# A streaming encoder layer: the down units placed behind the next row's first gate unit, and the first tiles' loads and splits cut into other pieces

## The chip, the cores and the metric

The kernel runs on one core of a Trainium2 chip. The time is device microseconds of that core for one execution, with inputs in HBM and outputs written back to HBM. The kernel before was timed in three runs. One further execution was taken by the profiler; all rows below are from that one.

## What is computed

One layer of a hybrid encoder is applied to 544 tokens: 512 of a prompt and 32 of a running stream. All values are float32, D_MODEL is 1024 and D_FF is 2816.

```python
def mixer(xn, conv_prev, w_in, ln_g, ln_b, w_s, b_s, conv_w, w_pa, w_pb, w_o):
    z = xn @ w_in
    u_a, v_a, bg, cg, hh, ga, gb = jnp.split(z, SPLIT_IDX, axis=-1)
    u = jax.nn.gelu(u_a, approximate=False)
    v = layernorm(jax.nn.gelu(v_a, approximate=False), ln_g, ln_b)
    a = u * spatial_gate(v, w_s, b_s)
...
    m = jax.nn.sigmoid(ga) * (a @ w_pa) + jax.nn.sigmoid(gb) * (bconv @ w_pb)
    return m @ w_o, xc[:, -(CONV_WIDTH - 1):], v

def swiglu(x, w_gate, w_up, w_down):
    return (jax.nn.silu(x @ w_gate) * (x @ w_up)) @ w_down

def trunk(x, ...):
        x = x + mo
        x = x + swiglu(rmsnorm(x, norm_ffn[l]), w_gate[l], w_up[l], w_down[l])
    return rmsnorm(x, norm_final), ...
```

The first product that runs is v_A = rmsnorm(x) @ W_in for the columns of v. The swiglu is the "ffn" and "down" phases of the kernel, and the last rmsnorm is its tail.

## The kernel before

**Layout.** Activations lie with features on the 128 partitions and the 544 tokens along the free dimension, in two halves of 272. Each float32 operand is split into a high part (`w_hi`, `act_hi`, made by a cast on ScalarE) and a low remainder (`w_lo`, `act_lo`, a subtraction on VectorE), and each product is three matmuls: high by high, high by low, low by high.

**Head.** SyncE issues, in this order, the scale columns `cols64`, the first block of x, and then pieces of the first weight unit between the other x blocks (`load_x`, `load_first`: four pieces of two 128-row blocks each, read from `w_in` in rows of 1 KB). ScalarE makes the high parts (`take_x`, `first_unit`) and VectorE the low ones. TensorE meanwhile runs `keep_busy(WARM)`: 14 matmuls of ones, each seen in the trace as two passes. Then it takes the K blocks one by one (`step(k, i, h)`): 12 matmuls for each block k. Each needs `x_ready` of that block and `first_lo` of the weights' piece.

**Units of seven products.** The projections behind the mixer and most of the feed-forward part run as units. A unit takes 1 MB of weights as four quadrants and forms seven products of sums of quadrants with sums of token halves and blocks (in place of eight). Each product is 4 blocks by 3 matmuls, so a unit is 84 matmuls. VectorE makes the sums of the weights (`sums_of_b`: one instruction at L1759 and two at L1763). ScalarE casts them (`form`, L1144), and VectorE subtracts (`form`, L1773). All forms of unit n+1 are made while TensorE works on unit n. ScalarE also copies the banks of products 0, 1, 2 and 4 out of PSUM (`copy_part`, L1155). TensorE needs these copies at products 2, 3, 4 and 6. Within a unit ScalarE's order is fixed: copy 0 and form 0, copy 1, copy 2 and form 2, form 3 where it stands alone, copy 4 and form 4, form 5, form 6. A copy behind a form waits for that form.

**The order of the feed-forward units** is the tuple `FFN`. There are 11 pairs of a gate unit and an up unit, in three rows of 4, 4 and 3 pairs (`PAIRS`). Behind each of the first two rows come four down units, which take that row's h = silu(gate) * up. The last row's down product is the separate phase "down". Units are numbered n = 0 to 29 here: 0 to 7 are the first row's gates and ups, 8 to 11 its downs, 12 to 19 the second row, 20 to 23 its downs, 24 to 29 the third row. h of a pair is turned into its seven operand forms during the next gate unit: the "split" work in `gate`, 8 instructions of VectorE between its own. A row's last pair has no gate behind it. Its eight instructions stand at the head of `down` for m = 0, and TensorE has a function of its own for that unit, `first_down`: it takes the known three blocks of products 0, 1 and 5 first, and then the fourth.

**From the feed-forward units to the phase "down".** At L2287 VectorE makes the low parts of the weights. Ahead of it stands a wait for `gf_all` (the final norm's weights, whose load waits for the last unit's `form_used`). ScalarE loads its table for the square root (L1488) ahead of its cast at L1477.

**Tail.** The last block of x is done in two token parts (`LAST`). For each part ScalarE squares (L1503), takes the root (L1505) and scales one row block (L1509). TensorE turns the block (L1008) and adds up the squares (L1024). VectorE ends the norm and scales the rest, and SyncE stores.

## Times and profile before

| | us |
|---|---|
| median of 3 runs | 856.38 |
| lowest and highest run | 855.93, 857.24 |
| the profiled execution | 856.78 |
| its span, first to last instruction | 854.7 |
| TensorE busy in it | 841.1 (98%) |
| VectorE busy | 700.1 (82%) |
| ScalarE busy | 448.2 (52%) |

The span leaves out 2.1 us of the profiled execution's time, which lie around it. In the trace a stretch where TensorE has nothing to run is idle time, with what ended it. The start of one matmul to the start of the next tells more exactly what was lost, since the ends are modelled.

### The profile page before, as it was taken

What the parts mean: (1) busy time and instruction counts of PE and PEld (TensorE: products, weight loads), DVE (VectorE), ACT (ScalarE), POOL (GpSimd) and SP (SyncE); (2) the same over time, 40 slices, a digit from 0 to 9 for tenths busy, and PEclk for the clock granted to TensorE, in tenths of its full rate; (3) what the DMA queues carried; (4) which work ended last, traced back from release to release, by engine and by line L of the source; (5) the groups of instructions that cost most, each with busy time, mean ns of one, the idle gap of its engine ahead of it and who ended that gap; (6) DMA issues with size and microseconds to landing.
All of it is one profiled execution on the core that took longest, in us unless ns stands there. A gap on an engine that the chain in (4) does not pass through costs nothing.

```text
span 854.7 us, 16297 instructions
## 1 busy us (share of the span) xinstructions
PE 841.1 (98%) x6654; PEld 837.7 (98%) x6654; DVE 700.1 (82%) x1098; ACT 448.2 (52%) x766; POOL 17.4 (2%) x23
## 2 busy tenths in 40 slices
PE   9999999999999999999999999999999999999996
PEld 9999999999999999999999999999999999999996
DVE  6768878789898989845578899999999999888545
ACT  7432225556566565651256776654566655466422
POOL 0000000000000000000000000000000000000031
PEclk9999999999999999999999999999999999999998
DMA  8333314132333232231542122222222222222322
GB/s 300 114 100 102 105 51 151 50 107 99 108 97 110 93 112 98 96 126 50 178 134 90 51 99 100 99 99 99 100 99 100 99 97 101 99 99 69 93 61 105
DMA packets 39496, 88.49 MB, mean 104 GB/s; under 512 B 2177, under 2 KB 28801, under 8 KB 33025
## 3 DMA queue, kind: packets, MB, share of 16 engines
q1 hardware_dynamic: 39424, 87.49, 30.3%
q8 instruction: 52, 0.85, 0.4%
q14 instruction: 20, 0.16, 0.1%
HBM read 85.10 MB, written 2.38 MB: 102 GB/s over the span
## 4 chain that ended last, share of the span: by engine, by line
PE 95%; DVE 2%; ACT 1%; DMA 0%; issue 0%; POOL 0%; DVEq 0%; ACTq 0%; POOLq 0%
PE ps_main L836 13%; PE ps_main L837 12%; PE ps_main L838 12%; PE ps_main L641 10%; PE ps_main L639 10%; PE ps_main L640 10%; PE ps_t L836 7%; PE ps_t L837 7%; PE ps_t L838 7%; PE ps_g L782 1%; PE ps_g L684 1%; DVE w_lo L1773 1%; ACT w_hi L1144 1%; PE ps_t L666 1%; DMA gf_all<-in_norm_final_dram 0%
## 5 line engine op out<-in xcount | busy, mean ns | idle before, releaser
L836 PE MATMUL ps_main<-xf_hi,w_hi 128*128 128x272 f32 x756 | 218.6, 289 | 0.0
L837 PE MATMUL ps_main<-xf_lo,w_hi 128*128 128x272 f32 x756 | 218.5, 289 | 0.0
L838 PE MATMUL ps_main<-xf_hi,w_lo 128*128 128x272 f32 x756 | 218.4, 289 | 0.0
L639 PE MATMUL ps_main<-act_hi,w_hi 128*128 128x272 f32 x692 | 201.1, 291 | 0.9 <-DVE w_lo L2287 0.9
L641 PE MATMUL ps_main<-act_hi,w_lo 128*128 128x272 f32 x692 | 200.0, 289 | 0.0
L640 PE MATMUL ps_main<-act_lo,w_hi 128*128 128x272 f32 x692 | 199.1, 288 | 0.0
L1773 DVE TENSOR_TENSOR w_lo<-w_sums,w_hi 128x1024 fp32r<-128x1024 f32 x150 | 129.6, 865 | 26.4 <-ACT w_hi L1144 25.7
L1144 ACT CAST w_hi<-w_sums 128x1024 fp32r<-128x1024 f32 x150 | 113.9, 760 | 57.4 <-DVE w_sums L1763 35.9
L836 PEld LDWEIGHTS ps_main<-xf_hi,w_hi 128*128 128x128 f32 x756 | 142.4, 188 | 0.0
L838 PEld LDWEIGHTS ps_main<-xf_hi,w_lo 128*128 128x128 f32 x756 | 142.3, 188 | 0.0
L837 PEld LDWEIGHTS ps_main<-xf_lo,w_hi 128*128 128x128 f32 x756 | 142.2, 188 | 0.0
L639 PEld LDWEIGHTS ps_main<-act_hi,w_hi 128*128 128x128 f32 x692 | 130.3, 188 | 1.3 <-issue 1.1
L640 PEld LDWEIGHTS ps_main<-act_lo,w_hi 128*128 128x128 f32 x692 | 130.4, 188 | 0.0
L641 PEld LDWEIGHTS ps_main<-act_hi,w_lo 128*128 128x128 f32 x692 | 130.1, 188 | 0.0
L836 PE MATMUL ps_t<-xf_hi,w_hi 128*128 128x272 f32 x420 | 121.6, 290 | 0.0
L837 PE MATMUL ps_t<-xf_lo,w_hi 128*128 128x272 f32 x420 | 121.4, 289 | 0.0
L838 PE MATMUL ps_t<-xf_hi,w_lo 128*128 128x272 f32 x420 | 121.3, 289 | 0.0
L1773 DVE TENSOR_TENSOR w_lo<-w_raw,w_hi 128x1024 fp32r<-128x1024 f32 (+1 forms) x104 | 95.9, 922 | 5.2 <-ACT w_hi L1144 4.9
L1144 ACT CAST w_hi<-w_raw 128x1024 fp32r<-128x1024 f32 (+1 forms) x104 | 83.9, 807 | 15.1 <-PE ps_t L838 9.7
L836 PEld LDWEIGHTS ps_t<-xf_hi,w_hi 128*128 128x128 f32 x420 | 79.1, 188 | 0.4
L838 PEld LDWEIGHTS ps_t<-xf_hi,w_lo 128*128 128x128 f32 x420 | 79.0, 188 | 0.0
L837 PEld LDWEIGHTS ps_t<-xf_lo,w_hi 128*128 128x128 f32 x420 | 79.0, 188 | 0.0
(281 smaller groups left out, 1288.6 us busy)
## 6 DMA issues: line engine op xcount, KB each, us to landing
w_raw<-in_w_quads_dram SPq DMA_DIRECT2D x20, 1024.0 KB, 4.9
w_raw<-in_w_gate_dram SPq DMA_DIRECT2D x11, 1024.0 KB, 4.9
w_raw<-in_w_up_dram SPq DMA_DIRECT2D x11, 1024.0 KB, 4.9
w_raw<-in_w_down_quads_dram SPq DMA_DIRECT2D x8, 1024.0 KB, 4.9
w_raw<-in_w_in_dram SPq DMA_DIRECT2D x6, 1024.0 KB, 5.1
w_raw<-in_w_pa_dram SPq DMA_DIRECT2D x4, 1024.0 KB, 5.4
w_raw<-in_w_pb_dram SPq DMA_DIRECT2D x4, 1024.0 KB, 5.2
w_raw<-in_w_o_dram SPq DMA_DIRECT2D x4, 1024.0 KB, 6.7
```

The source lines that it names most:

```text
L639: pe.matmul(out, whi, xhi, start=(opens and k == order[0]), stop=False)
L640: pe.matmul(out, whi, xlo, start=False, stop=False)
L641: last = pe.matmul(out, wlo, xhi, start=False, stop=(closes and k == order[-1]))
L666: last = pe.transpose(dst, src[:, c * P:c * P + ROWS[c]], ident[:, :])
L684: pe.matmul(ps_g[:, 1, 0:P], ones[:, :], ones[:, :], start=True, stop=True)
L782: pe.matmul(ps_g[:, 0, c * P:(c + 1) * P], tok[:, c, group], ws_t[:, g, :], start=True, stop=True)
L836: pe.matmul(out, whi, xhi, start=opens and k == 0, stop=False, skip_group_check=not opens)
L837: pe.matmul(out, whi, xlo, start=False, stop=False, skip_group_check=not opens)
L838: last = pe.matmul(out, wlo, xhi, start=False, stop=k == KQ - 1, skip_group_check=not opens)
L1144: act.copy(f_hi[:, form_group(q, f), :], form_source(q, f, s)).then_inc(third_hi if f == 3 else form_hi, 1)
L1773: dve.tensor_tensor(f_lo[:, group, :], form_source(q, f, s), fbits(f_hi[:, group, :]), ALU.subtract).then_inc(third_lo if f == 3 else form ...
```

## The change

The order of the feed-forward units becomes a function, `ffn_units`: each row's four down units now stand behind the **gate unit of the next row's first pair**, and the up unit of that pair behind them. So the row's last h is made in a gate unit, as that of every other pair. `first_down`, `parts_first` and the head of `down` for m = 0 are gone. The gate's result lies in `gate_sb` over the four down units.

At the head, x's first block is issued ahead of `cols64`, and both of its splits are done in two token halves. The first weights come in five pieces of 1, 1, 2, 2 and 2 blocks, from an input of their own that holds each partition's row in one piece. `WARM` goes from 14 to 9. One addition of squares moves behind a split.

Ahead of the phase "down", the wait for `gf_all` moves behind the first uses, and the first cast ahead of the table load. In the tail, ScalarE squares the second part ahead of scaling the first part's rows.

```diff
+def ffn_units():
+    order = []
+    for c, pairs in enumerate(PAIRS):
+        for n in range(pairs):
+            order.append(("gate", c, n))
+            if c and n == 0:
+                order += [("down", c - 1, m) for m in range(4)]
+            order.append(("up", c, n))
+    return tuple(order)
...
-    WARM = 14
+    WARM = 9
+    FIRST = ((0, 1), (1, 2), (2, 4), (4, 6), (6, 8))
...
-    ALONE = [0, QG] + [QG + n for n, (kind, _, m) in enumerate(FFN) if kind == "down" and m == 0]
+    ALONE = [0, QG]
...
             def load_first(n):
-                dst = w_raw[:, 0, n * 4 * P:(n + 1) * 4 * P].rearrange("p (k n) -> p k n", k=2)
-                src = row_blocks(w_in, slice(2 * n * P, 2 * (n + 1) * P), V0, 2 * P)
-                sp.dma_start(dst, src).then_inc(first_loaded[n], 16)
+                at = slice(FIRST[n][0] * 2 * P, FIRST[n][1] * 2 * P)
+                sp.dma_start(w_raw[:, 0, at], w_first[:, at]).then_inc(first_loaded[n], 16)
+            load_x(0)
             sp.dma_start(cols64[:], cols).then_inc(cols_loaded, 16)
-            load_x(0)
             load_first(0)
             load_x(1)
+            load_first(1)
             load_x(2)
-            load_first(1)
+            load_first(2)
...
+                weights(0)
+                for h in range(2):
+                    pe.wait_ge(x_ready, h + 1)
+                    for i in range(2):
+                        step(0, i, h)
+                for k in range(1, KD - 2):
+                    pe.wait_ge(x_ready, k + 2)
+                    weights(k)
...
+                def h_there(x, k):
+                    if k == KQ - 1:
+                        pe.wait_ge(hf_ready, h_made + {A11: 2, A12: 2, A22: 2, S3: 3, S1: 3, S2: 4, S4: 5}[x])
...
-                if kind == "down" and m == 0:
-                    first_down(QG + n, n % 2, c)
-                elif n >= 2:
+                if n >= 2:
                     seven(QG + n, n % 2, behind=...,
                           forms=h_forms if kind == "down" else x_forms,
+                          h_made=5 * (KQ * c + KQ - 1) if kind == "down" and m == 0 else None)
...
-                elif kind == "down" and m == 1:
+                elif kind == "down" and m == 0 and f == 2:
                     act.wait_ge(hf_ready, 5 * KQ * (c + 1))
...
-                split, plain = m and c < 2, m and c == 2
+                split, plain = n and (c < 2 or m == 0), m and c == 2
...
             act.wait_ge(silu_done, NF)
             act.activation(root[:, 0:1], msq[:, 0:1], ACT.Sqrt).then_inc(root_done, 1)
-            split_down(p, 0, 0, NF2)
...
-            dve.wait_ge(gf_loaded, 16)
             split_down(p, 0, 1, NF2)
             take_x2(0, 0, first=True)
             split_down(p, 0, 0, NF2)
             take_x2(0, 1, first=True)
+            dve.wait_ge(gf_loaded, 16)
...
+            last_squares(0)
+            last_root(0)
+            last_squares(1)
+            last_scale(0)
+            last_root(1)
+            last_scale(1)
```

In the changed kernel `split_down(p, 0, 0, NF2)` stands ahead of the `silu_done` wait. Between the last up unit of a row and the first down unit, VectorE's order is as follows. Before, from the last up unit's final form into the first down unit (`w_lo` and `w_sums` are a unit's forms and sums, `hf_lo` and `s_lo` are h's low parts):

```order
L2069 TENSOR_TENSOR up_sb<-ps_t,gate_sb 128x544
L2084 TENSOR_TENSOR gate_sb<-up_sb 128x544
L1773 TENSOR_TENSOR w_lo<-w_raw,w_hi 128x512
L2115 TENSOR_TENSOR hf_lo<-up_sb,hf_hi 128x272
L2090 SCALAR_TENSOR_TENSOR up_sb<-gate_sb,up_sb 128x272
L2108 TENSOR_TENSOR hf_lo<-up_sb,hf_hi 128x2x272
L2122 TENSOR_TENSOR hf_lo<-gate_sb,hf_hi 128x2x272
L2098 SCALAR_TENSOR_TENSOR up_sb<-up_sb 128x272
L2129 TENSOR_TENSOR hf_lo<-up_sb,hf_hi 128x272
L2136 TENSOR_TENSOR s_lo_121<-up_sb,s_hi_117 128x272
L1773 TENSOR_TENSOR w_lo<-w_sums,w_hi 128x512 x2
L1759 TENSOR_TENSOR w_sums<-w_raw 128x1024
```

After, the same place, now a gate unit:

```order
L2075 TENSOR_TENSOR up_sb<-ps_t,gate_sb 128x544
L1765 TENSOR_TENSOR w_sums<-w_raw 128x1024
L2090 TENSOR_TENSOR gate_sb<-up_sb 128x544
L1779 TENSOR_TENSOR w_lo<-w_raw,w_hi 128x512
L2112 TENSOR_TENSOR hf_lo<-up_sb,hf_hi 128x2x272
L1769 TENSOR_TENSOR w_sums<-w_sums,w_raw 128x512
L2096 SCALAR_TENSOR_TENSOR up_sb<-gate_sb,up_sb 128x272
L2119 TENSOR_TENSOR hf_lo<-up_sb,hf_hi 128x272
L1769 TENSOR_TENSOR w_sums<-w_sums,w_raw 128x512
L2102 SCALAR_TENSOR_TENSOR up_sb<-up_sb 128x272
L1779 TENSOR_TENSOR w_lo<-w_sums,w_hi 128x1024
```

The sums of the next unit's weights (L1759, now L1765) stood behind h's whole chain and now stand ahead of it, with the rest of the chain between them.

On VectorE at the head of the program, before (the splits of x, `act_lo`, and of the first weights, `w_lo`):

```order
L1563 SCALAR_TENSOR_TENSOR act_lo<-resid,cols_61,act_hi 128x544
L1569 TENSOR_TENSOR w_lo<-w_raw,w_hi 128x512
L1563 SCALAR_TENSOR_TENSOR act_lo<-resid,cols_61,act_hi 128x544 x2
L1569 TENSOR_TENSOR w_lo<-w_raw,w_hi 128x512
L1563 SCALAR_TENSOR_TENSOR act_lo<-resid,cols_61,act_hi 128x544 x2
```

and after:

```order
L1566 SCALAR_TENSOR_TENSOR act_lo<-resid,cols_61,act_hi 128x272
L1572 TENSOR_TENSOR w_lo<-w_raw,w_hi 128x256
L1566 SCALAR_TENSOR_TENSOR act_lo<-resid,cols_61,act_hi 128x272
L1566 SCALAR_TENSOR_TENSOR act_lo<-resid,cols_61,act_hi 128x544
L1572 TENSOR_TENSOR w_lo<-w_raw,w_hi 128x256
L1566 SCALAR_TENSOR_TENSOR act_lo<-resid,cols_61,act_hi 128x544
L1572 TENSOR_TENSOR w_lo<-w_raw,w_hi 128x512
```

The first matmul needs the first two of these rows in both kernels. Each of them is now half as wide, and the third block's weights come two rows later.

On ScalarE in the tail, before (squares, root, scaled rows, for the first part and then for the second):

```order
L1503 ACTIVATE y_sq<-x_last 128x256
L1505 ACTIVATE root<-msq 128x2
L1509 ACTIVATE y_tok<-y_tok,rstd 128x1024
L1503 ACTIVATE y_sq<-x_last 128x288
L1505 ACTIVATE root<-msq 128x3
```

and after:

```order
L1492 ACTIVATE y_sq<-x_last 128x256
L1498 ACTIVATE root<-msq 128x2
L1492 ACTIVATE y_sq<-x_last 128x288
L1505 ACTIVATE y_tok<-y_tok,rstd 128x1024
L1498 ACTIVATE root<-msq 128x3
```

The second part's squares, for which TensorE waits, moved ahead of one scaling of 1024 columns.

## Rows read from the trace of the kernel before

**Rows 1.** The profile's first line.

```profile
span 854.7 us, 16297 instructions
```

**Rows 2.** Waits of TensorE: engine line waited for: total us, times, longest.

```profile
PE ps_main L836 <- ACT parts L1155: 3.1, 2, 1.6
...
PE ps_main L639 <- DVE w_lo L2287: 0.9, 1, 0.9
...
PE ps_main L1024 <- ACT y_sq L1503: 0.4, 1, 0.4
```

**Rows 3.** Timeline of TensorE (start, us, line): first matmuls of units 8 to 11, 19, 20.

```profile
564.97 0.29 PE L836 MATMUL ps_main<-hf_hi,w_hi 128*128 128x272 f32 x1
...
577.69 0.29 PE L836 MATMUL ps_t<-hf_hi,w_hi 128*128 128x272 f32 x1
...
588.40 0.29 PE L836 MATMUL ps_main<-hf_hi,w_hi 128*128 128x272 f32 x1
...
598.97 0.29 PE L836 MATMUL ps_t<-hf_hi,w_hi 128*128 128x272 f32 x1
...
683.69 0.29 PE L836 MATMUL ps_t<-xf_hi,w_hi 128*128 128x272 f32 x1
...
694.47 0.29 PE L836 MATMUL ps_main<-hf_hi,w_hi 128*128 128x272 f32 x1
```

**Rows 4.** Timelines of VectorE (first sums) and ScalarE, units 5 to 10.

```profile
537.07 1.22 DVE L1759 TENSOR_TENSOR w_sums<-w_raw 128x1024 f32<-128x1024 f32 x1
...
546.26 1.22 DVE L1759 TENSOR_TENSOR w_sums<-w_raw 128x1024 f32<-128x1024 f32 x1
...
558.44 1.22 DVE L1759 TENSOR_TENSOR w_sums<-w_raw 128x1024 f32<-128x1024 f32 x1
...
574.68 1.05 ACT L1144 CAST w_hi<-w_sums 128x1024 fp32r<-128x1024 f32 x1 [2.72 <-DVE w_sums L1763]
575.63 0.39 ACT L1155 ACTIVATE parts<-ps_main 128x272 f32<-128x272 f32 x1
...
582.94 1.22 DVE L1759 TENSOR_TENSOR w_sums<-w_raw 128x1024 f32<-128x1024 f32 x1
...
593.19 1.22 DVE L1759 TENSOR_TENSOR w_sums<-w_raw 128x1024 f32<-128x1024 f32 x1
```

**Rows 5.** Timelines of the head, by engine.

```profile
0.82 0.40 SPq L510 DMA_DIRECT2D cols<-in_cols_dram  x1
...
1.69 6.03 PE L684 MATMUL ps_g<-ones 128*128 128x128 f32 x28 [1.69 <-POOL ident L2413]
...
7.48 0.37 PE L694 MATMUL ps_main<-act_hi,w_hi 128*128 128x272 f32 x1
...
4.24 0.75 ACT L1051 ACTIVATE act_hi<-resid,cols 128x544 fp32r<-128x544 f32 x1 [1.94 <-DMA resid<-in_x_t_dram]
5.76 0.62 ACT L1058 CAST w_hi<-w_raw 128x512 fp32r<-128x512 f32 x1 [0.77 <-DMA w_raw<-in_w_in_dram]
...
7.58 0.75 ACT L1051 ACTIVATE act_hi<-resid,cols 128x544 fp32r<-128x544 f32 x1 [0.38 <-DMA resid<-in_x_t_dram]
...
6.42 0.69 DVE L1569 TENSOR_TENSOR w_lo<-w_raw,w_hi 128x512 fp32r<-128x512 f32 x1 [0.52 <-ACT w_hi L1058]
...
9.07 0.69 DVE L1569 TENSOR_TENSOR w_lo<-w_raw,w_hi 128x512 fp32r<-128x512 f32 x1
```

**Rows 6.** Timelines around the start of the phase "down".

```profile
808.02 0.39 PE L639 MATMUL ps_main<-act_hi,w_hi 128*128 128x272 f32 x1 [0.89 <-DVE w_lo L2287]
...
804.14 1.28 ACT L1488 ACT_TABLE_LOAD   x1
...
806.92 0.96 DVE L2287 TENSOR_TENSOR w_lo<-w_raw,w_hi 128x768 fp32r<-128x768 f32 x1 [2.04 <-DMA gf_all<-in_norm_final_dram]
```

**Rows 7.** The tail: stretches, busy us by engine, clock, DMA share, GB/s.

```profile
850.00:851.00 1.00, 0.00 (x0) 0.00 (x0) 0.78 (x2) 0.45 (x1) 0.00 (x0) 0.67 0.64 240
851.00:852.00 1.00, 0.00 (x0) 0.00 (x0) 0.00 (x0) 0.00 (x0) 0.00 (x0) 0.50 1.06 402
```

More of the change, by code:

```diff
@@ L81 @@
 PAIRS = (4, 4, 3)
-FFN = tuple((kind, c, n) for c, pairs in enumerate(PAIRS)
-            for kind, n in [(kind, n) for n in range(pairs) for kind in ("gate", "up")] + [("down", n) for n in range(4 if c < 2 else 0)])
+def ffn_units():
[7 more added lines that the diff above has]
+    return tuple(order)
+FFN = ffn_units()
 class Phase:
@@ L704, in first_unit @@
                             step(k, i, h)
-                pe.wait_ge(first_lo, KD // 2)
+                weights(KD - 2)
                 for i in range(2):
@@ L825, in h_forms, with product @@
                 return (s4_hi[k][:], s4_lo[k][:]) if x == S4 else (hf_hi[:, x, k, :], hf_lo[:, x, k, :])
-            def product(q, s, f, blocks, forms, there=None, opening=(0, 1), used=1):
+            def product(q, s, f, blocks, forms, there=None):
                 _, _, x, bank = PRODUCTS[f]
-                out, opens = banks[s][bank], f in opening
+                out, opens = banks[s][bank], f < 2
                 for k in blocks:
@@ L838, in product, with seven @@
                     last = pe.matmul(out, wlo, xhi, start=False, stop=k == KQ - 1, skip_group_check=not opens)
-                if blocks[-1] == KQ - 1 and used:
-                    last.then_inc(form_used, used)
-            def seven(q, s, first=None, behind={}, bank_b=None, forms=x_forms):
+                last.then_inc(form_used, 1)
+            def seven(q, s, first=None, behind={}, bank_b=None, forms=x_forms, h_made=None):
                 def there(x, k):
                     pe.wait_ge(xf_ready, NPROD * (first + k) + X_ORDER.index(x) + 1)
+                def h_there(x, k):
+                    if k == KQ - 1:
+                        pe.wait_ge(hf_ready, h_made + {A11: 2, A12: 2, A22: 2, S3: 3, S1: 3, S2: 4, S4: 5}[x])
                 for f in range(NPROD):
@@ L1451, in seven @@
                             up_free(n, f)
-                        copy_part(q, s, f, first=parts_first[:] if kind == "down" and m == 0 else None)
+                        copy_part(q, s, f)
                     else:
@@ L2224, in up @@
                 second_sums(q, 1, up_sb)
-                if not last and QG + n + 1 in ALONE:
-                    next_form(n, 3)
                 second_rest(q, 1, up_sb)
@@ L2229, in up @@
                 scale_second(q, up_sb, gate_sb[:, 1, :], h_made)
-                if not last and QG + n + 1 not in ALONE:
+                if not last:
                     next_form(n, 4)
```

169 lines of the change are left out of this document (64 added, 105 removed).

## The prediction

> **What bounds the kernel now.** First the span [rows 1] against TensorE's busy time: 841.1 of 854.7 us. TensorE is the bound, and its matmuls stay the same in number and shape apart from the warm-up. So only its gaps count, and the work ahead of its first real matmul and behind its last. Second, who made it wait [rows 2]: two long waits for ScalarE's copy at L1155, one for VectorE's weights at L2287, one for the squares at L1503. Third, the timeline of TensorE, by the starts of whole units, since a lost interval shows there in full. A down unit without trouble takes 598.97 - 588.40 = 10.57 us [rows 3], or 84 matmuls at 0.126 us. The first down unit takes 577.69 - 564.97 = 12.72 us; the one of the second row has the same length, so there are two. Fourth, why it does [rows 4]: in the first down unit VectorE works off the eight instructions of h before it makes the next unit's sums. ScalarE's cast of these sums starts at 574.68, 9.71 us into the unit, after idling 2.72 us for them. The copy of product 4 stands behind that cast and ends at 576.02, and TensorE has waited for it since 574.5. That is the 1.55 us of the long wait; short waits for h's parts make up the rest.
>
> **The change, part by part.**
>
> *Down units behind a gate unit.* Removed: 12.72 - 10.57 = 2.15 us, twice, 4.30 us. What is late next? VectorE is nearly full here, so I follow when it starts a unit's sums, measured from TensorE's start of that unit. Its own pace comes from the distances of L1759 [rows 4]: from an up unit to the gate 546.26 - 537.07 = 9.19 us, from a gate with h's work to the up 558.44 - 546.26 = 12.18, from down to down 593.19 - 582.94 = 10.25. In unit 7 (start 564.97 - 10.62 = 554.35) the sums start at +4.09. The new gate unit has the work of the old ones. With units of 10.6 us, its sums start at 4.09 + 9.19 - 10.6 = +2.7, those of the first down unit behind it at 2.7 + 12.18 - 10.6 = +4.3. Each further down gains 0.3. Which lateness costs? Before, down unit 9 has +5.25 (582.94) and takes 588.40 - 577.69 = 10.71 us, so it loses 0.14. Unit 10 has +4.79 (593.19) and takes 10.57, so it loses nothing [rows 3, 4]. At +4.3 the new first down is inside, and the 0.14 goes too. The up unit ahead of the second row's downs took 694.47 - 683.69 = 10.78 us, 0.21 too long, with one form cast by itself which now falls away. The second row enters some 0.15 later than the first (two cycles of 9.19 + 12.18 against two of 10.6, over four pairs, less what idle time takes back), so at about +4.5, still inside. Sum: 4.30 + 0.14 + 0.21 = **4.65 us**. The addition of `parts_first` (one of 272 columns) falls away on VectorE and was hidden. The loads on SyncE's queue keep their number and their waits. Down unit 0 now puts its copies into the upper half of `up_sb`, where h lay, so ScalarE's copy of product 2 waits for h's last low part. By the split work's place in the gate before, that ends about 2 us into the down unit, and the copy's data exist at 4.5 us. If it were late, the forms behind it on ScalarE, and then TensorE, would be late by the same.
>
> *Start of the phase "down".* VectorE waited 2.04 us for `gf_all` and TensorE 0.89 us for VectorE [rows 6]. Without that wait, the next bound is ScalarE's cast. It now stands ahead of the table load of 1.28 us at 804.14, so it ends at about 804.14 + 0.82 = 805.0, and VectorE's 0.96 us ends at 806.0. TensorE wants the weights at about 807.0. Nothing is late. The gain is 0.89 us, and at most 1.1 with the slower restart (a first matmul of 0.39 us). I take **1.0**. The table load moves into ScalarE's idle time ahead of the second cast, and `gf_all`, there by 806.9, is first used some 6 us later.
>
> *Tail.* The squares of the second part no longer stand behind the scaling, so TensorE's last wait of 0.4 us [rows 2] goes. The scaled rows are ready about 0.9 us later and the root right behind them just in time. The stores, though, fill the DMA engines: they are at 0.64 from 850 to 851 and full after that [rows 7]. The last stores can come forward only into that 0.36 us. Bounds 0 and 0.45, value **0.3**.
>
> *Head.* The first matmul starts at 7.48 [rows 5]. Its chain was: piece 0 landed at 5.76, cast 0.62, low part from 6.42 in 0.69, that is 7.11, then the end of the 28 warm-up passes (6.03 us from 1.69). In the new kernel x's first block is issued 0.46 us sooner (at 0.82, the place of `cols64`). Piece 0 holds half, and the time from block to piece, 5.76 - 4.24 = 1.52, may halve, so it lands between 4.5 and 5.3. Half-width splits cost between half and all of 0.62 and 0.69; by their halves the first matmul can start at about 5.6, and 6.5 is the other bound. The 18 passes end at 1.69 + 18/28 x 6.03 = 5.6. But that is not the gain. TensorE next needs the third block's weights, which arrive in the same order and amount of data as before: low part at 9.07 + 0.69 = 9.76, and ScalarE was already waiting for data at 7.58 (0.38 us). They can be earlier by 0 to 0.46. TensorE reached that block at 7.48 + 24 x 0.126 = 10.5. So the head gains 10.5 - 9.76 = 0.7 to 1.2 us, and I take **0.95**; what comes earlier is spent waiting ahead of block 1 or 2. Block 0 in two halves adds one instruction each to ScalarE and VectorE, some 0.1 us of cover that is there. The moved addition of squares only lets a weight split go first.
>
> The warm-up's passes took 6.03 / 28 = 0.215 us each, while the real matmuls of twice their columns run at 0.126 from 7.7 on: the array was at 1.2 GHz until about then and at 2.4 GHz after it. The new kernel starts real work while it may still be at 1.2 GHz. Until 7.5 this costs nothing that counts, since 24 matmuls fit between 5.6 and 9.6 with half of that time at the lower level. By the Trainium skill's page "TensorE: Matmul & The Clock Gate" (Part 1: The HAM clock gate), the lower clock is the default state and only activity releases it, so a shorter warm-up with a gap behind it may delay the release. This speaks against `WARM` 9; what it would give is the first rival below.
>
> **Sum.** 4.65 + 1.0 + 0.3 + 0.95 = 6.9 us. The profiled execution took 856.78, its span being 854.7, so it would take 849.9 with a span of 847.8. It was 0.4 above the median of 856.38. Against the median the forecast is **849.5 us**.
>
> **Rivals.** (1) *The clock rises late.* A gap between the 18 passes and the first matmul leaves the array at 1.2 GHz until past block 1. The 24 matmuls then take 24 x 0.25 = 6.0 us from 5.6, block 2 starts at 11.6 rather than 10.5, and the head loses 1.1 in place of gaining 0.95: 851.5. For it: the first piece may land 0.8 us later than I take. Against: the work is nearly unbroken from 1.69. (2) *The stall moves.* If the gate with h's work behind a full row leaves VectorE later than my +4.3, the first downs pay what lies beyond +4.8, and at the +7.3 of the old first down all of the 4.3 comes back: 853.8; at +5.3, some 0.3: 849.8. For it: 12.18 is longer than a unit. Against: 9.19 ahead of it. (3) *Slower.* VectorE becomes the bound over the down units: their 10.25 us cycle (with the scaling of `resid` in the first row) stands only 0.32 below the unit's 10.57. If the new order (gate result to scale, copies in the other buffers) made each of the eight downs wait as long as the old first one, 1.55 us, that is 12.4 us: 849.5 + 12.4 = 861.9. It turns the change into a loss from 6.9 / 8 = 0.86 us per down unit on, a cycle of 11.4. Nothing in the rows shows such a cycle. (4) *The head does nothing*, because data land as late as before: 850.5.
>
> **How the numbers follow.** Forecast with its small variants 0.68 (848.4 to 850.6), rival 1 0.11, rival 2 0.10, rival 3 0.03, rival 4 0.08. The range goes from 848.2 (head 1.2, start of "down" 1.1, tail 0.45, and runs that differ by 0.6) to 851.8, past rivals 4 and 1. Below 0.2% (1.7 us, about what a measurement can tell from no change) falls nearly nothing. Faster 0.96, same 0.01, slower 0.03.
>
> **What would show it.** In the changed kernel's trace: the first matmul at 5.4 to 6.5, and the third block's at 9.3 to 9.8, with a gap ahead of block 1 or 2 (else rival 1 or 4); all units of the feed-forward part at 10.6, the two first downs too, and the sums of a first down at about +4.3 (rival 2 if beyond +4.8); no wait of TensorE at the start of "down"; the last squares right behind VectorE's last block, and stores with no gap between them. The prediction is wrong if a wait for a copy at the old L1155 remains in a down or gate unit, or if the blocks 2 to 7 of the head come in later than before.

## The result, and the profile after

| | before | after |
|---|---|---|
| median, us | 856.38 | 852.13 |
| lowest and highest of 5 runs | 855.93, 857.24 | 851.88, 852.22 |
| ratio of the medians, 95% interval | | 0.9949 (0.9935 to 0.9962) |
| span of the profiled execution | 854.7 | 850.1 |
| first matmul on x's squares, from the start ("head") | 25.67 | 26.21 |
| from there to the first matmul of the last block ("middle") | 812.84 | 807.04 |
| from there to the end ("tail") | 16.22 | 16.85 |

The kernel is 4.25 us faster. Forecast were 6.9, so 852.13 lies just above the range of 848.2 to 851.8. The three parts of the span say where: the middle gained 5.80 (forecast 4.65 + 1.0 = 5.65), the head lost 0.54 (forecast: a gain of 0.95), and the tail lost 0.63 (forecast: a gain of 0.3). The two marks of the changed kernel:

```profile
26.21 0.59 PE L738 MATMUL ps_t<-r_x,ones 128*128 128x512 f32 x1
...
833.25 0.36 PE L986 MATMUL ps_main<-act_hi,w_hi 128*128 128x256 f32 x1
```

**The middle.** TensorE's waits, to be read against [rows 2]:

```profile
PE ps_g L697 <- POOL ident L2401: 1.7, 1, 1.7
PE ps_main L707 <- DVE w_lo L1572: 0.8, 1, 0.8
PE ps_g L998 <- DVE x_last L2332: 0.5, 1, 0.5
PE ps_g L688 <- ACT r_diag L1344: 0.2, 1, 0.2
```

The waits for copies, for the weights of "down" and for the last squares are gone. One is new: 0.8 us for `w_lo`, and it lies in the head. The first matmuls of the gate unit 8, of down units 9 and 10, of the up unit behind them, and of down units 21 and 22 (TensorE's timeline, as in [rows 3]):

```profile
565.49 0.29 PE L858 MATMUL ps_main<-xf_hi,w_hi 128*128 128x272 f32 x1
...
576.08 0.29 PE L858 MATMUL ps_t<-hf_hi,w_hi 128*128 128x272 f32 x1
...
586.65 0.29 PE L858 MATMUL ps_main<-hf_hi,w_hi 128*128 128x272 f32 x1
...
618.35 0.29 PE L858 MATMUL ps_t<-xf_hi,w_hi 128*128 128x272 f32 x1
...
703.09 0.29 PE L858 MATMUL ps_t<-hf_hi,w_hi 128*128 128x272 f32 x1
...
713.66 0.29 PE L858 MATMUL ps_main<-hf_hi,w_hi 128*128 128x272 f32 x1
```

The two first downs take 586.65 - 576.08 = 10.57 and 713.66 - 703.09 = 10.57 us, where they took 12.72. All four downs of the row take 618.35 - 576.08 = 42.27 = 4 x 10.57, and the gate unit ahead takes 10.59. VectorE's first sums of these two units, and ScalarE's cast of the first ones:

```profile
580.34 1.21 DVE L1765 TENSOR_TENSOR w_sums<-w_raw 128x1024 f32<-128x1024 f32 x1
...
707.53 1.22 DVE L1765 TENSOR_TENSOR w_sums<-w_raw 128x1024 f32<-128x1024 f32 x1
...
582.78 1.05 ACT L1138 CAST w_hi<-w_sums 128x1024 fp32r<-128x1024 f32 x1 [1.51 <-DVE w_sums L1769]
```

The sums come at +4.26 and +4.44 (forecast +4.3 and +4.5), the cast at +6.70, against +9.71 before [rows 4]. At the start of "down" the cast (799.91) now stands ahead of the table load (800.76), VectorE's low part is done at 801.74, and TensorE's matmuls follow each other at 0.126 us throughout.

Cut at the first matmul behind the feed-forward units (802.45 before, 798.33 after), the middle shows its two terms apart. From the squares to that matmul it takes 776.78 us before and 772.12 after, a gain of 4.66 (forecast 4.65). From there to the last block it takes 36.06 and 34.92, a gain of 1.14 (forecast 1.0, at most 1.1). That matmul before, and after:

```profile
802.45 0.29 PE L639 MATMUL ps_main<-act_hi,w_hi 128*128 128x272 f32 x1
```

```profile
798.33 0.29 PE L652 MATMUL ps_main<-act_hi,w_hi 128*128 128x272 f32 x1
```

**The head.** SyncE's first issues, and the weights' pieces on ScalarE and VectorE up to TensorE's third block (to be read against [rows 5]):

```profile
0.82 0.40 SPq L515 DMA_DIRECT2D resid<-in_x_t_dram  x1
1.28 0.42 SPq L523 DMA_DIRECT2D cols<-in_cols_dram  x1
1.75 0.42 SPq L520 DMA_DIRECT2D w_raw<-in_w_first_dram  x1
...
3.93 0.52 ACT L1041 ACTIVATE act_hi<-resid,cols 128x272 fp32r<-128x272 f32 x1 [1.63 <-DMA cols<-in_cols_dram]
4.94 0.41 ACT L1048 CAST w_hi<-w_raw 128x256 fp32r<-128x256 f32 x1 [0.48 <-DMA w_raw<-in_w_first_dram]
...
9.55 0.62 ACT L1048 CAST w_hi<-w_raw 128x512 fp32r<-128x512 f32 x1 [1.38 <-DMA w_raw<-in_w_first_dram]
...
10.20 0.69 DVE L1572 TENSOR_TENSOR w_lo<-w_raw,w_hi 128x512 fp32r<-128x512 f32 x1 [1.17 <-ACT w_hi L1048]
```

```profile
5.86 0.59 PE L707 MATMUL ps_main<-act_hi,w_hi 128*128 128x272 f32 x1
6.25 0.43 PE L708 MATMUL ps_main<-act_lo,w_hi 128*128 128x272 f32 x1
6.47 0.43 PE L709 MATMUL ps_main<-act_hi,w_lo 128*128 128x272 f32 x1
...
9.93 0.29 PE L709 MATMUL ps_main<-act_hi,w_lo 128*128 128x272 f32 x1
11.04 0.36 PE L707 MATMUL ps_main<-act_hi,w_hi 128*128 128x272 f32 x1 [0.82 <-DVE w_lo L1572]
```

The first matmul starts at 5.86, 1.6 us sooner than before. But the third block's weights reach ScalarE at 9.55, after a wait of 1.38 us for data, and are ready at 10.89. Before that was 9.76. TensorE has finished two blocks by 10.06 and starts the third at 11.04. What the early start won is spent waiting, and half a microsecond more.

**The tail.** VectorE's last scalings, then the stores (their sizes and the median time from issue to landing):

```profile
843.70 1.53 DVE L2373 TENSOR_SCALAR y_tok<-y_tok,rstd 128x512 f32<-128x512 f32 x3 [0.27 <-DVE rstd L2363]
...
out_dram<-y_tok SPq DMA_DIRECT2D x3, 512.0 KB, 3.4
out_dram<-y_tok SPq DMA_DIRECT2D x2, 256.0 KB, 2.8
out_dram<-y_tok SPq DMA_DIRECT2D x1, 128.0 KB, 4.1
```

Before, these stores took 3.3, 2.2 and 3.2 us. And ahead of the scalings VectorE is idle for 0.27 us with its own result at hand.

### The profile page after: what moved, and what is told of

It reads as the page before. It is cut to its first block, busy times and chain, and to the rows that moved or that the text cites. A ratio compares the mean times of both kernels' runs of the same rounds, so it can differ in the third digit from the quotient of the medians.

```text
span 850.1 us, 16275 instructions
## 1 busy us (share of the span) xinstructions
PE 838.9 (99%) x6644; PEld 836.4 (98%) x6644; DVE 698.8 (82%) x1096; ACT 448.7 (53%) x766; POOL 18.1 (2%) x23
## 4 chain that ended last, share of the span: by engine, by line
PE 97%; DMA 1%; ACT 1%; DVE 0%; SPq 0%; issue 0%; DVEq 0%
PE ps_main L858 13%; PE ps_main L859 13%; PE ps_main L860 13%; PE ps_main L654 10%; PE ps_main L652 10%; PE ps_main L653 10%; PE ps_t L858 7%; PE ps_t L859 7%; PE ps_t L860 7%; PE ps_g L804 1%; DMA w_raw<-in_w_first_dram 1%; PE ps_t L679 1%; PE ps_g L679 0%; PE ps_main L707 0%; PE ps_main L709 0%; PE ps_main L708 0%
## 5 line engine op out<-in xcount | busy, mean ns | idle before, releaser
L1779 DVE TENSOR_TENSOR w_lo<-w_raw,w_hi 128x512 fp32r<-128x512 f32 (+1 forms) x102 | 95.6, 937 | 5.1 <-ACT w_hi L1138 4.8
L1138 ACT CAST w_hi<-w_raw 128x512 fp32r<-128x512 f32 (+1 forms) x102 | 83.5, 819 | 16.8 <-PE ps_t L860 10.8
```

Of the source, the lines that this page charges most:

```text
L1138: act.copy(f_hi[:, form_group(q, f), :], form_source(q, f, s)).then_inc(third_hi if f == 3 else form_hi, 1)
L1779: dve.tensor_tensor(f_lo[:, group, :], form_source(q, f, s), fbits(f_hi[:, group, :]), ALU.subtract).then_inc(third_lo if f == 3 else form ...
```

## The experiments

Kernels of one group ran on one chip, with runs of the kernel before between them. The kernel before itself, timed in group 4 once more as a kernel of its own, came out at a ratio of 1.0005 (0.9996 to 1.0014), its median 0.46 us from that of its own runs. So differences under half a microsecond between medians mean little by themselves. The marks inside the profiled executions are finer for the middle and the tail: the changed kernel's two executions (the first one and `e0_after_again`) agree there to 0.01 us, and the two of the kernel before to 0.30 in the middle and 0.01 in the tail. Of the head that isn't so. The same two differ by 0.35 us there (26.21 and 25.86), and the two of the kernel before by 0.56 (25.67 and 25.11).

**Group 1: the changed kernel again, the whole head undone, and its parts.** `e0_after_again` is the changed kernel. `e1_head_before` takes back the head:

```diff
-            load_x(0)
             sp.dma_start(cols64[:], cols).then_inc(cols_loaded, 16)
+            load_x(0)
-    WARM = 9
-    FIRST = ((0, 1), (1, 2), (2, 4), (4, 6), (6, 8))
+    WARM = 14
+    FIRST = ((0, 2), (2, 4), (4, 6), (6, 8))
-            take_x(0, slice(0, HALF))
+            take_x(0)
             first_unit(0)
-            take_x(0, slice(HALF, N))
-                sp.dma_start(w_raw[:, 0, at], w_first[:, at]).then_inc(first_loaded[n], 16)
+                sp.dma_start(dst, row_blocks(w_in, slice(k0 * P, k1 * P), V0, 2 * P)).then_inc(first_loaded[n], 16)
```

`e3_rows_of_w_in` has only the last of these edits. `e4_four_pieces` has only the four pieces, in before's order among the x blocks.

> The changed kernel itself once more, as the measure for the others of this set. If what its first profile showed is the kernel's own: the third block's weights land at about 9.5 us, its first matmul starts at about 11.0, TensorE reaches the sum of x's squares at 26.2 (25.7 before), and the span ends 8.7 us after the last squares are summed (7.6 before). If the late landing and the long stores were chance of one execution, block 3 starts at 9.3 to 9.8 and the time is 849.5 to 850.5.

> The changed kernel with the whole head of before: the scale columns first, four pieces of two blocks in 1 KB rows of w_in, x's first block split whole, 14 warm-up matmuls. Theory that the new head costs 0.5 us: the first matmul at 7.5, no wait behind it, the squares' sum reached at 25.7, time 0.5 us below the changed kernel (851.6). Rival, that the head is neutral and the shift comes with the execution: no difference over 0.2 us.

> The changed kernel with its five pieces read from w_in in 1 KB rows, all else as changed. Theory that the new layout of the source makes the landings late (rows of one 8 KB row per partition, 2 KB per packet): the third block's weights land at 8.0 to 8.3 in place of 9.5, its matmuls start at 9.5 to 9.8, time 1.2 us below the changed kernel (850.9). Rival, that order and number of the pieces do it: still 9.3 to 9.6, time within 0.3 us of the changed kernel. Theory of the clock: no difference either.

> The changed kernel with four pieces of two blocks each from the new input, x's first block still ahead of the scale columns and split in halves. Theory of the layout: the second piece still lands after 9 us, time within 0.3 us of the changed kernel. Rival, the extra DMA and the queue position of the third block's piece (3.63 in place of 3.20): it lands 0.4 to 1.3 us sooner than 9.5, and the time is 0.4 to 1.2 us below the changed kernel, though the first matmul comes 0.4 us later.

| kernel | median (range), us | third block starts | head | tail |
|---|---|---|---|---|
| before, same chip | 856.29 | | | |
| e0, changed kernel | 851.86 (851.75 to 851.98) | 10.70 | 25.86 | 16.85 |
| e1, head of before | 850.62 (850.28 to 850.99) | 9.94 | 25.04 | 16.46 |
| e3, first weights from `w_in` | 851.16 (850.97 to 851.79) | 10.61 | 25.77 | 16.87 |
| e4, four pieces | 852.90 (851.16 to 854.47) | 10.61 | 25.70 | 16.47 |

The new head as a whole costs 851.86 - 850.62 = 1.24 us: 0.82 in the head and, unforeseen, 0.39 in the tail. Reading from `w_in` gives 0.70 of that back in the median; its profiled execution was its slowest (851.79), so its marks show little of it. The first piece with 256 KB from the new input is worse than with 128: its cast starts at 6.08, against 4.94 in e0 and 4.99 in e1, whose piece has 256 KB too but comes from `w_in`. Single runs of e4 lie up to 3.3 us apart.

**Group 2: before's head plus one of the new edits.** Each is e1 with one thing more: `e5_x_first` issues x's first block ahead of `cols64`, `e6_five_pieces` takes five pieces from `w_in`, `e7_warm_9` has 9 warm-up matmuls. `e9_head_tail_before` has before's order of ScalarE in the tail too:

```diff
             last_squares(0)
             last_root(0)
-            last_squares(1)
             last_scale(0)
+            last_squares(1)
```

> The changed kernel with the head of before (which gave 850.6), and of the new head only x's first block issued ahead of the scale columns. Theory that the order of the first two DMAs upsets the loads behind them: the third block starts at 10.3 or later in place of 9.9, the squares' sum is reached at 25.5 or later in place of 25.0, time 851.0 to 851.5. Rival, that the number of pieces does it: x's first block is cast 0.3 to 0.45 us sooner, nothing later, time within 0.2 us of 850.6.

> The changed kernel with the head of before, and of the new head only the five pieces of 1, 1, 2, 2 and 2 blocks (in 1 KB rows of w_in). Theory that the fifth DMA delays the third block's piece and, by the stores' place on the DMA engines, the end: third block at 10.4 or later, the end 8.7 us after the last squares in place of 8.3, time 851.2 to 851.9. Rival of the order of x and the columns: third block at 9.9, time within 0.2 us of 850.6.

> The changed kernel with the head of before, and of the new head only 9 warm-up matmuls in place of 14. Theory of the data: the first matmul waits for the first piece all the same and starts at 6.5, time within 0.2 us of 850.6. Rival of the clock: the array stays at its lower level for longer (0.226 us a matmul in blocks 0 and 1), the squares' sum comes up to 1 us later, time 851.0 to 851.6.

> The changed kernel with the head and ScalarE's tail order of before. Theory that the new tail order saves the wait of 0.5 us but the stores bunch up: the last squares come 0.5 us later (8.64 us after the last block's start in place of 8.13), the end is 7.6 us behind them in place of 8.3, time 0.2 us below 850.6. Rival, that the long stores come from an instruction load among them and not from the order: the end stays 8.3 us behind them, time 0.5 us above 850.6.

| kernel | median (range), us | first matmul | head | tail |
|---|---|---|---|---|
| e5, x first | 851.14 (850.57 to 851.33) | 6.97 | 25.18 | 16.46 |
| e6, five pieces | 850.74 (850.49 to 851.50) | 6.52 | 24.98 | 16.47 |
| e7, `WARM` 9 | 850.32 (850.28 to 850.58) | 6.62 | 24.84 | 16.47 |
| e9, before's tail order | 850.75 (850.44 to 851.49) | 6.82 | 25.04 | 16.64 |

None of the three costs 0.8 us by itself. e6 has the third block's weights as in the changed kernel, behind one piece more and issued at 3.63 rather than 3.20, and its third block starts at 9.61, sooner than e1's. The shorter warm-up is no loss. The new order of the tail is worth 16.64 - 16.46 = 0.18 us here, which a median can't show.

**Group 3: pairs, and the halves.** `e8_halves` is e1 with the token halves kept. `e10_x_first_five` is e5 and e6 together, `e11_five_warm_9` e6 and e7 together. `e12_whole_x` is the changed kernel with only the halves undone.

> The changed kernel with the head of before (first weights from w_in in four pieces, the scale columns first, 14 warm-up matmuls), except that the splits of x's first block stay in two token halves. Theory A (the halves carry the loss: ScalarE's and VectorE's extra pieces stand ahead of the later blocks, and the tail's instructions come 0.25 us later): x's squares sum at 25.4 to 25.9 (25.04 in e1), last sums to the end of the span 8.7 us in place of 8.3, median 851.3 to 851.8. Theory B (the halves cost nothing by themselves, the loss comes from the first piece of 128 KB together with x issued ahead): within 0.25 of e1's 850.6, the sum of squares at 25.0, last sums to the end 8.3.

> The changed kernel with before's head, except for two of the new edits together: x's first block issued ahead of the scale columns, and five pieces of 1, 1, 2, 2, 2 blocks (read from w_in). x's first block is split whole, 14 warm-up matmuls. Theory A (x first, by itself +0.5 us against e1, is what delays the pieces; five pieces only bring weights earlier): the sum of x's squares at 25.1 to 25.3, median 851.0 to 851.3. Theory B (the two edits hurt only together, the small first piece being taken early and the third block's weights late, with a wait ahead of block 2): third block at 10.3 or later, median 851.4 to 851.9. If the halves are the cause, it stays at 850.6 to 851.0.

> The changed kernel with before's head, except for 9 warm-up matmuls and five pieces read from w_in. Alone these gave 850.32 and 850.74 where the plain head of before gave 850.62. Theory A (each moves the first matmuls a little, and the third block's weights at 9.3 to 9.4 are early enough in both): 850.2 to 850.6, first matmul 6.4 to 6.6, third block 9.5 to 9.8, sum of x's squares at 24.8 to 25.0. Theory B (a short warm-up with an early first piece keeps the array at the lower clock longer, as in the changed kernel): blocks 0 and 1 at 0.2 us a matmul or more until about 7.8, third block at 10.0 or later, 850.9 to 851.5.

> The changed kernel with one edit undone: x's first block is split whole, not in token halves. All the rest of the new head stays (x first, 9 warm-up matmuls, five pieces from their own input). Theory A (the halves carry the loss at the head and the 0.25 us later scalings in the tail): last sums to the end 8.3, sum of x's squares at 25.3 to 25.6, median 851.0 to 851.4. Theory B (the loss comes from the order and size of the transfers): as the changed kernel, 851.6 to 852.1, wait for the third piece of 0.8 us or more on ScalarE, the third block at 10.5 or later. The first matmul goes from 5.86 to about 6.2 in both.

| kernel | median (range), us | third block | head | tail | instructions of VectorE |
|---|---|---|---|---|---|
| e8, halves | 850.55 (850.33 to 851.15) | 9.95 | 25.04 | 16.47 | 1095 |
| e10, x first, five pieces | 851.75 (850.65 to 852.02) | 10.23 | 25.33 | 16.45 | 1095 |
| e11, five pieces, `WARM` 9 | 850.73 (850.64 to 850.83) | 10.27 | 25.36 | 16.46 | 1095 |
| e12, whole x | 851.74 (851.54 to 852.02) | 10.79 | 25.95 | 16.46 | 1095 |

The halves cost the head nothing (e8) and e12 keeps the late head without them. Yet in e12 the tail falls back from 16.85 to 16.46. Nothing in the tail was edited. What differs is the count: a tail of 16.45 to 16.47 stands in all kernels in which VectorE runs 1094 or 1095 instructions (e9's other order apart), 16.85 to 16.87 in those with 1096 (after, e0, e3). e10 is split: two runs at 850.65 and 850.92, three at 851.75 to 852.02, and the profile is of one of the early ones. What its late runs look like isn't known.

**Group 4: the base, the order of the first two loads, and the count.** `e13_before_again` is the kernel before. `e14_cols_first` is the changed kernel with `cols64` first again. `e15_two_more_dve` is e1 with two fills more on VectorE, `e16_eight_more_dve` the changed kernel with eight, done while it is idle at the start:

```diff
+            for i in range(8):
+                dve.memset(newton[i % 2 * 64:i % 2 * 64 + 64, i // 2:i // 2 + 1], 0.0)
             dve.wait_ge(stats_set, 3)
```

> The kernel before, unchanged, for a second profiled execution. Theory A (the profiled execution that the prediction started from had a late head: first piece at 5.76 and sum of x's squares at 25.67, against 4.9 to 5.0 and 25.04 in the kernels with the same head): first piece's cast at 4.8 to 5.2, sum of x's squares at 25.0 to 25.3, last block to the end 16.2, span 854.0 to 854.3. Theory B (the execution was typical, and the kernels with the same head are early for another reason): 25.5 or later, span 854.5 or more.

> The changed kernel with one edit undone: the scale columns are issued ahead of x's first block again, as before. Halves, five pieces from their own input and 9 warm-up matmuls stay. Theory A (x ahead of the columns is the cause of the head's loss: in all six kernels with the columns first the DMA engines move 289 to 346 GB/s from 4 to 8 us, with x first 256 to 324): sum of x's squares at 25.0 to 25.4, third block at 10.2 or sooner, GB/s from 4 to 8 us 290 or more, median 850.9 to 851.4 (the tail's part of the loss stays). Theory B (the own input of the first weights, rows of 2048 bytes in place of 1024, slows the transfers): as the changed kernel, 25.8 to 26.2, 851.7 to 852.2, 270 GB/s or less.

> The changed kernel with the whole head of before (as e1), and two instructions more at the head of VectorE's program: fills of 64 partitions by one column, done while VectorE is idle. VectorE then has as many instructions as in the changed kernel. Theory A (the 0.27 us of idle ahead of VectorE's last scalings, seen in exactly the kernels with two instructions more than e1, hang on its count of instructions and not on its data): the idle time of 0.27 appears ahead of the last scalings, which start 10.45 us behind the last block's start and not 10.21, last block to the end 16.8 in place of 16.4, median 850.8 to 851.1. Theory B (they come with the halves or pieces of the head for another reason): no such idle time, 16.4, median 850.4 to 850.8.

> The changed kernel with eight instructions more at the head of VectorE's program (fills of 64 partitions by one column, done while VectorE is idle). Theory A (count of instructions): the idle time of 0.27 us moves away from the last scalings to an instruction some eight earlier in the tail, where it may be hidden; the last scalings start 10.2 us behind the last block's start, last block to the end 16.4 to 16.5, median 851.4 to 851.8. Theory B: all as in the changed kernel, 10.45, 16.85, median 851.9 to 852.2.

| kernel | median (range), us | head | tail | instructions of VectorE |
|---|---|---|---|---|
| e13, before | 856.40 (855.94 to 856.98) | 25.11 | 16.23 | 1098 |
| e14, columns first | 852.49 (851.85 to 852.74) | 25.87 | 16.84 | 1096 |
| e15, e1 and two fills | 851.03 (850.72 to 851.26) | 25.28 | 16.86 | 1096 |
| e16, after and eight fills | 851.41 (851.11 to 851.45) | 26.41 | 15.89 | 1104 |

The second execution of the kernel before has its head at 25.11, not 25.67: the one that the prediction started from was 0.56 late there. e14 clears the order of the first loads: x ahead of the columns isn't what the changed kernel loses by. e15 settles the tail. Two fills of 64 partitions by one column, 840 us ahead of it, make the idle time appear and the tail 0.40 longer:

```profile
842.79 1.53 DVE L2374 TENSOR_SCALAR y_tok<-y_tok,rstd 128x512 f32<-128x512 f32 x3 [0.27 <-DVE rstd L2364]
```

Eight fills take it away again, and 0.96 us with it. The DMA view shows where that comes from. From 838 to 848 us, in e16, and then in the changed kernel (each number of the GB/s line is a fortieth of the stretch, 0.25 us):

```profile
GB/s 0 0 0 0 0 0 0 0 0 0 0 0 0 0 0 33 0 0 229 410 393 393 410 410 442 393 410 360 385 369 393 369 401 377 443 393 442 377 410 295
...
q14 instruction: 1, 0.01, 0.3%
```

```profile
GB/s 0 0 0 0 0 0 0 0 0 0 0 0 0 0 0 0 0 213 426 377 410 393 410 393 426 410 393 344 262 393 369 336 401 426 483 352 434 360 377 262
...
q14 instruction: 1, 0.01, 0.2%
```

Either stretch has one load of instructions, of 8192 bytes. In e16 it stands alone at 841.8 (the 33), ahead of the stores. In the changed kernel it falls among them, at 845.3. By the packets' times, nine of the loads after the start lie 1.8 to 8.6 us earlier in e16 than in the changed kernel, while the others keep their place to 0.5 us, but for the very last (0.7 us earlier). So those nine, and this one among them, hang on VectorE's program. Counted from the last block's start, this load comes at 8.4 us in both executions of the kernel before, at 8.3 in e16 and at 12.1 in the changed kernel.

**Group 5: the layout of the new input, and the best of all parts.** `e17_blocks_of_own` is e14 with the first weights' own input as 1024 rows of 256 columns. A piece is then rows of 1 KB, as from `w_in`, and no longer stretches out of a row of 8 KB for each partition:

```diff
-                sp.dma_start(w_raw[:, 0, at], w_first[:, at]).then_inc(first_loaded[n], 16)
+                sp.dma_start(dst, row_blocks(w_first, slice(k0 * P, k1 * P), 0, 2 * P)).then_inc(first_loaded[n], 16)
```

`e18_warm_9_eight_more` is e7, the fastest so far, with the eight fills.

> As e14 (the changed kernel with the scale columns issued first again), but the first weights' own input holds them as 1024 rows of 256 columns, one 128-row block behind the other, so that a partition's part of a piece of two blocks is two rows of 1 KB as in w_in, and no longer one stretch of 2 KB out of a row of 8 KB. Theory A (the layout by partitions slows the transfers: pieces of 1 to 2 KB at a distance of 8 KB): 290 GB/s or more from 4 to 8 us, third block at 10.3 or sooner, sum of x's squares at 25.0 to 25.4, median 850.9 to 851.4. Theory B (it is the second input as such, wherever its rows lie): 270 GB/s or less, 25.8, median 851.8 to 852.7 as e14.

> The changed kernel with the head of before but 9 warm-up matmuls (as e7, the fastest so far at 850.32), and eight instructions more at the head of VectorE's program (as e16, whose tail was 0.9 us shorter than the changed kernel's: last block to the end 15.9). Theory A (the load of 8192 bytes that e16 moved from 845 to 842, ahead of the stores, is worth some 0.5 us against e7's tail of 16.47, and e7's head is unchanged): last block to the end 15.9 to 16.1, median 849.7 to 850.0, faster than both kernels. Theory B (e16's short tail came from its late head or by chance): last block to the end 16.4 or more, median 850.2 to 850.6.

| kernel | median (range), us | third block | head | tail |
|---|---|---|---|---|
| e17, own input by blocks | 851.08 (850.79 to 851.93) | 10.29 | 25.45 | 16.84 |
| e18, e7 and eight fills | 849.84 (849.62 to 849.94) | 9.83 | 24.93 | 15.88 |

With the layout changed, the median falls by 852.49 - 851.08 = 1.41 us against e14 and the head by 0.42. (The two ran on different chips, whose kernels before had medians of 855.94 and 855.91.) That speaks for the layout, though 0.42 is little more than two executions of one kernel differ by in the head. But the rate from 4 to 8 us didn't follow: e17's windows give 269 GB/s, which was the other theory's number. So by its median and its marks the layout seems to bear a part of the loss, and the mechanism that I had for it isn't shown.

That window in the changed kernel (busy us by engine, clock, DMA share, GB/s):

```profile
4.00:8.00 4.00, 4.00 (x19) 3.75 (x19) 2.21 (x5) 2.85 (x6) 0.00 (x0) 1.00 0.91 256
```

In e14, with the columns first:

```profile
4.00:8.00 4.00, 4.00 (x19) 3.91 (x19) 1.69 (x4) 2.53 (x6) 0.00 (x0) 1.00 0.93 266
```

In e3, with the first weights from `w_in`:

```profile
4.00:8.00 4.00, 3.35 (x21) 2.94 (x20) 2.55 (x5) 2.21 (x5) 0.00 (x0) 1.00 0.94 276
```

And in e1:

```profile
4.00:8.00 4.00, 4.00 (x31) 4.00 (x30) 1.90 (x3) 2.67 (x4) 0.00 (x0) 1.00 1.00 323
```

All seven kernels with the own input move 246 to 269 GB/s here. The thirteen that read `w_in` move 276 to 346, the kernel before among them with 289 and 316. But most of the thirteen have other parts of before's head too. e3, which differs from the changed kernel in the array alone, moves 276 against the 256 and 269 of that kernel's two executions. Per busy time the changed kernel moves 256 / 0.91 = 281 and e1 323, so its packets take longer. Against e1, the changed kernel has moved (323 - 256) x 4 + (223 - 217) x 2 = 280 KB less by 8 us; at the 370 GB/s of its next 4 us that is 0.76 us of the 1.10 by which its third block is later (11.04 against 9.94). The rest stays open. That the piece is issued later in the queue, behind one piece more, isn't it: e6 has just that.

Where the third block's weights are late shows most directly on ScalarE. First e6, the piece's issue and its cast, and then e3, the cast with the split of x ahead of it:

```profile
3.63 0.43 SPq L522 DMA_DIRECT2D w_raw<-in_w_in_dram  x1
...
7.81 0.62 ACT L1050 CAST w_hi<-w_raw 128x512 fp32r<-128x512 f32 x1
```

```profile
8.29 0.75 ACT L1043 ACTIVATE act_hi<-resid,cols 128x544 fp32r<-128x544 f32 x1 [1.20 <-DMA resid<-in_x_t_dram]
8.99 0.62 ACT L1050 CAST w_hi<-w_raw 128x512 fp32r<-128x512 f32 x1
```

This cast starts at 8.69 to 9.75 in all seven kernels with the own input, and in each of them ScalarE idles for just this piece (0.28 to 1.38 us). In twelve of the thirteen with `w_in` it starts at 7.81 to 8.36. The thirteenth is e3, at 8.99, where ScalarE waits 1.20 us for x's block and not for the weights. So the array that the first weights come from sorts the kernels, over all orders and sizes of the pieces. But e3 says that it isn't the whole: with `w_in` and all else of the new head, its third block still starts at 10.61.

e18 runs at a ratio of 0.9927 (0.9913 to 0.994) to the kernel before, which is 6.1 us, and 2.3 us below the changed kernel, on different chips. Its stores:

```profile
out_dram<-y_tok SPq DMA_DIRECT2D x3, 512.0 KB, 3.2
out_dram<-y_tok SPq DMA_DIRECT2D x2, 256.0 KB, 2.3
out_dram<-y_tok SPq DMA_DIRECT2D x1, 128.0 KB, 3.3
```

## Why the prediction was right and wrong

**Down units: right.** The gain of 4.65 (4.66) and the lateness of VectorE's sums (+4.3, +4.5) came out to within 0.06 us. The second execution of before (e13) gives 4.63. Copying the pace of a unit type from one place to another (9.19, 12.18, 10.25 from [rows 4]) was enough. Rival 2 asked for lateness beyond +4.8 and rival 3 for a cycle of 11.4; the downs' starts are 10.57 apart.

**Start of "down": right.** Forecast 1.0. It measured 1.14 against the execution of before and 0.87 against e13, in which TensorE had waited 0.6 us for the weights in place of 0.9. Together the middle gained 5.80 against the execution of before and 812.54 - 807.04 = 5.50 against the second one (e13), for a forecast of 5.65.

**Head: wrong, by 1.5 us.** Its steps have to be kept apart. The first matmul at "about 5.6" and piece 0 at 4.5 to 5.3 were right (5.86 and 4.94). That this isn't the gain was right too. The step that failed is the next one: "the third block's weights, which arrive in the same order and amount of data as before", and "can be earlier by 0 to 0.46". I looked for the cost of an edit to the transfers in their order and their bytes, and gave no bound below zero, while the source of each piece had changed. The data came 1.13 us later (10.89 against 9.76), and the third block started at 11.04 where 9.3 to 9.8 was forecast, one of the prediction's own signs of being wrong. Of the reason the runs show a part: the kernels with the own input have this piece late, and the later issue behind one more piece costs nothing by itself (e6). Why the own input is late, and why e3 is late without it, stays open. Rival 4 has the head do nothing, but it still missed the loss. The second failure is the base: the profiled execution had its first piece at 5.76, the second execution at 5.17 or sooner, and its head was 0.56 shorter. More than half of the gain of 0.95 read from [rows 5] was one execution's lateness. A single execution's head was taken for the kernel's. The sum then took the same 6.9 off the median, though that execution was 0.4 above it.

**The clock (rival 1): seen in part, and not the cause.** That its price of 851.5 lies near the result is chance. In the changed kernel the first matmuls are 0.22 to 0.23 us apart until 7.8 (the lower level, 1.2 GHz), and 0.126 after that. In e16 and e3 with the same 9 warm-up matmuls they are at 0.126 from 6.1 on, and e16's third block is at 11.24 all the same. e7 has `WARM` 9 without a loss, but its matmuls are at the higher level from the second one on (6.85), so it doesn't test a late rise. The changed kernel does: its array is at the higher level from 7.8 on, and it waits 0.82 us for the third block's weights all the same. The Trainium skill's page "TensorE: Matmul & The Clock Gate" (Part 1: The HAM clock gate) has the lower level as the state that the array starts in. The traces agree: the changed kernel's first real matmuls still run at it. But what a shorter warm-up may have delayed cost nothing here. TensorE was waiting for data either way.

**Tail: the mechanism right, the result covered.** Forecast 0.3. The last wait for squares went, and the last squares come 8.13 us behind the last block's start, where it was 8.64. With the instruction load ahead of the stores, as it was before the change, the tail takes 15.88 instead of 16.22 or 16.23: a gain of 0.3. In the changed kernel the load had moved among the stores (+0.59 us, e7 against e18, which differ in the eight fills alone) and VectorE had got a stall of 0.27 ahead of its last scalings (+0.39). The step that failed is the lower bound of 0: the term had no line for what the length of an engine's program does.

**The sum.** Forecast -6.9. Head +1.49, tail +0.93, middle -0.15 make -4.6, the difference of the two spans. The range's lower end adds up to 848.4 from its own parts (0.25, 0.1, 0.15 and 0.6 off 849.5), not to 848.2, but nothing hangs on that. With the head of before but for the shorter warm-up, and the load in its old place, the change's other parts give 849.84 (e18). That this lies near the 849.5 forecast for the whole says little: the gain against the same chip's runs of before is 6.1, not 6.9, and none of it comes from the head as it was forecast.

## What to carry to other kernels

When transfers already fill the DMA engines at the start of a kernel, a first piece that lands sooner moves only the first matmul. Read when the second and third blocks' data land, and bound that term below zero as well, above all when a load's source changes. Take a head from two profiled executions before pricing it. And where a kernel ends in stores, look for a load of instructions among them: a few instructions more or fewer ahead of it on an engine move it, so a change of half a microsecond in the tail may have nothing to do with the edit.

## What the runs showed of the hardware

- The time of an unedited stretch hangs on the number of instructions that an engine has run before it: tails of 16.46 us with 1094 or 1095 instructions on VectorE (with the new order of the tail), 16.85 with 1096, and 15.88 with 1102 or 1104. In each of the three groups the tails agree to 0.03 us.
- One instruction load of 8192 bytes (0.31 us on one of the DMA engines) among stores that fill all 16 goes with an end 0.59 us later than where it stands ahead of them (e7 against e18).
- From 4 to 8 us the DMA engines are all but fully busy and yet move 246 to 346 GB/s, against 334 to 401 from 8 to 12. It goes with the array that the first weights are read from: at most 269 from the new one in any kernel, at least 276 from the old, though the one kernel that differs from the changed one in nothing else has 276. The third block's weights are cast from 8.69 us on at the earliest with the new one, and by 8.36 with the old but for e3. Why is open. e17 speaks for the layout as a part of it, and shows that the rate in this window doesn't tell the whole.
- With the same 9 warm-up matmuls, real matmuls ran at the higher level from 6.1 us on in e3 and e16, and only from 7.8 or 7.9 in the changed kernel and e14. Of the eleven kernels with 9 warm-up matmuls, six ran real matmuls at the lower level, up to 7.2 to 7.9 us; of the nine with 14, whose real matmuls start later, none did. What decided it isn't known; the warm-up's length alone did not. The profile's granted clock reads 1.00 from 4 to 8 us in all of them, so here the level shows only in the distances of the matmuls. The same page of the Trainium skill (Part 1: The HAM clock gate) says that the moment of the rise differs from run to run. These traces hardly test it: the one kernel with two executions and a late rise has it at 7.8 and at 7.7.
